# Four of an expert's twelve weight chunks kept in a second place, loaded one expert ahead and moved by VectorE

## The chip, the cores and the metric

The kernel runs on one core of a Trainium2 chip. The metric is the device time of one execution in microseconds (us). The core has five engines with their own instruction streams: TensorE (PE; its weight loads are listed as PEld), VectorE (DVE), ScalarE (ACT), GpSimd (POOL) and SyncE (SP). They run side by side and meet at semaphores. Transfers are carried by 16 DMA engines; SP, ACT and POOL issue them.

## The reference

A transformer block with a mixture of experts, followed by a second block with two kinds of attention, on 512 tokens of width 1024, all in float32. Only the mixture of experts matters here:

```python
logits = (xt @ p['w_router'] + p['b_router']).astype(F32)   # 512 tokens, 32 experts
top_val, top_idx = lax.top_k(logits, TOP_K)                 # TOP_K = 4
gates = jax.nn.softmax(top_val, axis=-1)
...
def expert_block(args):
    e, x_b = args
    gu = x_b @ w_gu[e] + b_gu[e]                            # 1024 x 2048
    gate = jnp.minimum(gu[..., ::2], SWIGLU_LIMIT)
    up = jnp.clip(gu[..., 1::2], -SWIGLU_LIMIT, SWIGLU_LIMIT)
    return ((up + 1.0) * (gate * jax.nn.sigmoid(SWIGLU_ALPHA * gate))) @ w_dn[e] + b_dn[e]
```

Each token goes through four of the 32 experts, and the four results are summed with the gates as weights.

## The kernel before

**Blocks.** The kernel works on blocks of 64 token slots (`SLOTS`), each of one expert. An expert with more than 64 tokens has two or more blocks, one behind the other. The routing stage (`route_stage`, a chain of small VectorE operations) counts the tokens of each expert, orders the experts so that large and small ones alternate as evenly as they can, and writes a table: the expert of block v. For these inputs there are 47 blocks, and the numbers of blocks of the experts in their order are 1, 2, 1, 1, 2, 1, 2, 1, 1, 2, 1, 1, 2, 1, 2, 1, 1, 2, 1, 1, 4, 1, 2, 1, 1, 2, 1, 1, 3, 1, 2, 1: twelve experts with more than one block, twenty with one. (Blocks are counted from 1 in this document.)

**Weights.** An expert's weights are 12 MB, twelve chunks of 1 MB: 0 to 7 for gate and up (0 to 3 for half 0 of the columns, 4 to 7 for half 1), 8 to 11 for down. SBUF has room for one expert, one place for each chunk (`expert_w`). There is one semaphore `chunk{i}_arrived` for each chunk.

**The loop** (`experts`, stage `moe`). Each engine has a loop over the blocks, and `takes(engine, signal, n)` waits for a signal and takes it away again.

- SP (L1320 to 1327): for chunks 0 to 11, in this order, it waits until TensorE has used the chunk in this block, and then issues the load of the same chunk of the next block's expert. Where the next block has the same expert, the load is skipped and only its signal is given:

```python
for i in range(CHUNKS):
    takes(sp, s["last_used"] if i == CHUNKS - 1 else s["used"])
    sp.dma_start(w[:, i], weights.source[after, i], cond=(after != here)).then_inc(arrived[i], 16)
```

- TensorE (L1342 to 1393): gate and up, half 0 and half 1, chunk by chunk, each behind its `arrived` (L1353); the turn of the activation of half 0 (L1365) and of the next block's tokens (L1274); the down product of half 0 with chunks 8 and 9 (L1379); the turn of half 1 and its down product with chunks 10 and 11. The turns use the gated activation that VectorE makes.
- VectorE (L1433 to 1445): it spreads the bias with a shuffle (L1435), and for each half adds it to the product (L1439), clips, and multiplies gate and up with ScalarE's sigmoid into `act_sb` (L1445).
- ScalarE: the sigmoid (L1400), which loads its table in the first half; copies of the turned activation (L1404); the modulation of the next block's tokens (L1280); the copy of the down result `yb` (L1421) and its store; the load of the next bias.
- GpSimd: the gather of the next block's tokens (L1335).

The first expert's chunks are called for in the stage `ffn` (`load_first`), before the routing.

Of the kernel before, what the change touches and what calls it, by code (L numbers as in the profile page):

```python
# [15 lines left out]
F32 = mybir.dt.float32  # L16
# [6 lines left out]
P = 128  # L23
# [145 lines left out]
class LateModulation:  # L169
# [5 lines left out]
    def __init__(self, nc, held, ones):  # L175
        self.nc, self.ones = nc, ones
        self.cond = held.enter_context(nc.sbuf_tensor("late_cond_cols", [P, LATE, KD], F32))
        self.columns = held.enter_context(nc.sbuf_tensor("late_columns", [P, LATE * 4], F32))
# [454 lines left out]
def ffn_block(nc, d, g, ring, x, row_cols, ones):  # L633

    tiles = [x[:, m] for m in range(NT_X)]
    with ExitStack() as ffn:
        def sb(name, shape, dtype=F32):
            return ffn.enter_context(nc.sbuf_tensor(name, shape, dtype))

        gain, shift = sb("ffn_gain", [P, KD]), sb("ffn_shift", [P, KD])  # L640
        weight, slot_of = sb("weight_of", [P, NT_X, TOP_K]), sb("slot_of", [P, NT_X, TOP_K], U32)
        of_expert = sb("of_expert", [P, NT_X, N_EXP])
        token_of = sb("token_of", [P, LISTED], U32)
        table, n_blocks = sb("table", [1, P], I32), sb("n_blocks", [1, 1], I32)
        rows = nc.dram_tensor("normed_rows", (SEQ, D), F32).ap()
        y = sb("ffn_y", [P, NT_X, D])
        moving = ffn.enter_context(ExitStack())
        weights = ExpertWeights(nc, d, moving)
        routing = ffn.enter_context(ExitStack())
        hT = routing.enter_context(nc.sbuf_tensor("ffn_hT", [P, KD, SEQ], F32))  # L650
# [11 lines left out]
        norm_turn_stage(nc, "ffn", tiles, None, [y[:, m] for m in range(NT_X)], hT,  # L662
                        lambda m, k: (gain[:, k:k + 1], shift[:, k:k + 1]), g.eps_col[:, 0:1], g.ident[:, :],
                        early=weights.load_first)
        route_stage(nc, tables, g, hT, ones, y, rows, weight, slot_of, of_expert, token_of, table, n_blocks)
        routing.close()
        slot_rows = experts(nc, d, g, weights, rows, gain, shift, token_of, table, n_blocks)
        moving.close()
        combine(nc, d, g, slot_rows, weight, slot_of, of_expert, y)
        row = sb("ffn_row", [P, D])  # L670
        rows_stage(nc, g, "ffn_rows", [row_cols[:, 1]], [row[:, :]], ones)
        add_normed_stage(nc, g, "post_ffn", [y[:, m] for m in range(NT_X)], tiles, row[:, :],
                         early=lambda sp: ring.call_first(sp, second_weights(d)))

# [306 lines left out]
CHUNKS = 12  # L981
LIMIT, ALPHA = 7.0, 1.702
# [22 lines left out]
def route_stage(nc, tables, g, hT, ones, xn, rows, weight, slot_of, of_expert, token_of, table, n_blocks):  # L1005
# [6 lines left out]
    with ExitStack() as held:  # L1012
        def sb(name, shape, dtype=F32):
            return held.enter_context(nc.sbuf_tensor(name, shape, dtype))
# [27 lines left out]
        experti = sb("router_experti", [P, 1], I32)  # L1042
        ps = held.enter_context(nc.psum_tensor("router_ps", [P, NT_X, 512], F32))
        ps_r = held.enter_context(nc.psum_tensor("router_rank", [P, 1, 512], F32))
        with stage(nc, "route", "by_expert", "by_expert_kept", "logits", "negtop", "weight", "chosen", "rank", "chain", "expert",
                   "table", "slots", "hot", "listed", "rows", "at", "top", clear=(tables.loaded,)) as (s, block):
            @block.sync
            def _(sp):
                sp.wait_ge(s["expert"], 2)
                sp.dma_start(table[0:1, :], experti[:, 0:1]).then_inc(s["table"], 16)  # L1050
                sp.wait_ge(s["table"], 16)
# [43 lines left out]
            def _(dve):  # L1095
# [62 lines left out]
                step(nc.vector.tensor_scalar(many[:, 2:3], many[:, 2:3], -1.0, part[:, 0:1], ALU.add, ALU.min))  # L1158
# [5 lines left out]
                nc.vector.tensor_copy(experti[:, :], expert[:, 0:1]).then_inc(s["expert"], 1)  # L1164
# [65 lines left out]

def experts(nc, d, g, weights, rows, gain, shift, token_of, table, n_blocks):
# [9 lines left out]
    with ExitStack() as held:  # L1241
# [22 lines left out]
        carried = [stored, bias_here, gu_read, xg_free, xgT_made]  # L1264
# [20 lines left out]

        with stage(nc, "moe_start", "tokens", "xg_turned", "set", "rows_set", pool_dma=(gathered,)) as (s, block):
            @block.vector
            def _(dve):
                nc.vector.tensor_copy(tokens[:, :], token_of[:, 0:1]).then_inc(s["tokens"], 1)
                nc.vector.memset(yb[:, 0:1], 0.0).then_inc(gu_read, 2)  # L1290
                nc.vector.memset(yb[:, 1:2], 0.0).then_inc(stored, 32)
                nc.vector.memset(b_rows[:, :], 0.0).then_inc(s["rows_set"], 1)
# [21 lines left out]
        with stage(nc, "moe", "used", "last_used", "gu_made", "bias_free", "ga", "sig", "acted", "turned", "actT",  # L1314
                   "dn_made", "yb_made", "xg_here", "xg_turned", "copied", "step", pool_dma=(gathered,)) as (s, block):

            def takes(engine, signal, n=1):
                engine.wait_ge(signal, n).then_inc(signal, -n)  # L1318

            @block.sync  # L1320
            def _(sp):
                with sp.Fori(0, turns) as v:
                    here = sp.value_load(table[0:1, bass.ds(v, 1)], min_val=0, max_val=N_EXP - 1)
                    after = sp.value_load(table[0:1, bass.ds(v + 1, 1)], min_val=0, max_val=N_EXP - 1)
# [19 lines left out]
            def _(pe):  # L1344
# [26 lines left out]
                def down(half):  # L1371
                    takes(pe, s["actT"])
                    for q in range(2):
                        i = 8 + 2 * half + q
                        takes(pe, arrived[i], 16)
# [7 lines left out]
                        last.then_inc(s["used"] if i < CHUNKS - 1 else s["dn_made"], 1)  # L1383
# [13 lines left out]
            def _(act):  # L1397
# [9 lines left out]
                with act.Fori(0, turns) as v:  # L1407
                    here = act.value_load(table[0:1, bass.ds(v, 1)], min_val=0, max_val=N_EXP - 1)
                    after = act.value_load(table[0:1, bass.ds(v + 1, 1)], min_val=0, max_val=N_EXP - 1)
# [9 lines left out]
                    nc.scalar.sem_inc(s["last_used"], 1)  # L1419
# [8 lines left out]
            def _(dve):  # L1428
# [4 lines left out]
                with dve.Fori(0, turns):  # L1433
# [1473 lines left out]
def build_program(nc, d, out):  # L2907
    with ExitStack() as whole:
# [48 lines left out]
        ring = WeightRing(nc, "b2_w", whole)  # L2957
        ffn_block(nc, d, g, ring, x, row_cols, ones[:, :])
# [163 lines left out]
```

## Time and profile before

| | |
|---|---|
| runs | 3132.25 us median of 3 (3132.21 to 3143.58) |
| the profiled execution's own time | 3136.93 us |
| its span in the trace | 3135.1 us |
| granted TensorE clock, mean over the span | 0.912 |
| TensorE matmuls busy | 2613.1 us (83%) |
| VectorE busy | 1013.8 us (32%) |
| expert loop, from its first matmul to the last read of the down result | 1286.8 to 2436.2 us |
| bytes moved by DMA over the whole span | 553.36 MB |

The span runs from the first to the last instruction of one profiled execution. Busy shares are means over stages with different limits, so what matters for a change in the expert loop is read from the loop's own rows. In the rows further down, a timeline row gives the start, the length, the engine, the line and the operation; "x64" is the number of instructions merged, and the brackets tell how long the engine had been idle before and what ended that.

### The profile page before, as it was taken

What the parts mean: (1) busy time and instruction counts of PE and PEld (TensorE: products, weight loads), DVE (VectorE), ACT (ScalarE), POOL (GpSimd) and SP (SyncE); (2) the same over time, 40 slices, a digit from 0 to 9 for tenths busy, and PEclk for the clock granted to TensorE, in tenths of its full rate; (3) what the DMA queues carried; (4) which work ended last, traced back from release to release, by engine and by line L of the source; (5) the groups of instructions that cost most, each with busy time, mean ns of one, the idle gap of its engine ahead of it and who ended that gap; (6) DMA issues with size and microseconds to landing.
All of it is one profiled execution on the core that took longest, in us unless ns stands there. A gap on an engine that the chain in (4) does not pass through costs nothing. (4 is left out here: it accounts for less than half of the span.)

```text
span 3135.1 us, 51899 instructions
## 1 busy us (share of the span) xinstructions
PE 2613.1 (83%) x19294; PEld 1299.5 (41%) x19294; DVE 1013.8 (32%) x2284; ACT 764.4 (24%) x1726; POOL 346.5 (11%) x331
## 2 busy tenths in 40 slices
PE   6788686856789994699988989998999399679998
PEld 1446464645464442333333333333333154355444
DVE  1263636363155424322222222222222502443012
ACT  2133333343060002122222222222222201355000
POOL 0021212130060000000000000000000201244000
PEclk9888798977889997799999999999999599887999
DMA  5100000000307414499999999399968421001112
GB/s 203 57 26 23 6 23 6 23 2 3 108 28 281 147 67 183 184 390 387 387 391 390 387 395 422 150 384 411 402 269 360 148 90 64 19 2 55 54 56 79
DMA packets 114086, 553.36 MB, mean 177 GB/s; under 512 B 12912, under 2 KB 16496, under 8 KB 62352
## 3 DMA queue, kind: packets, MB, share of 16 engines
q1 hardware_dynamic: 97184, 510.27, 40.4%
q10 hardware_dynamic: 10608, 19.91, 1.9%
q0 software_dynamic: 6144, 20.98, 1.8%
q8 instruction: 119, 1.95, 0.3%
q14 instruction: 31, 0.25, 0.0%
HBM read 736.18 MB, written 16.52 MB: 240 GB/s over the span
## 5 line engine op out<-in xcount | busy, mean ns | idle before, releaser
L1353 PE MATMUL moe_gu_ps<-expert_w,xgT 128*64 128x512 f32 x3008 | 667.9, 595 | 39.3 <-PEq L1318 39.2
L1353 PEld LDWEIGHTS moe_gu_ps<-expert_w,xgT 128*64 128x64 f32 x3008 | 252.8, 137 | 445.5 <-issue 445.5
L1379 PE MATMUL moe_down_ps<-expert_w,actT 128*64 128x512 f32 x1504 | 344.6, 597 | 54.8 <-PEq L1318 54.8
L1439 DVE TENSOR_TENSOR biased<-moe_gu_ps,b_gu 128x512 f32<-128x512 f32 x94 | 65.0, 692 | 615.7 <-DVEq L1318 615.7
L1379 PEld LDWEIGHTS moe_down_ps<-expert_w,actT 128*64 128x64 f32 x1504 | 116.7, 136 | 222.2 <-issue 222.2
L1400 ACT ACT_TABLE_LOAD x47 | 60.3, 1283 | 383.0 <-ACTq L1318 383.0
L1868 PE MATMUL ahead_ps<-hT,x 128*128 128x256 f32 (+1 forms) x288 | 128.1, 542 | 5.8 <-PEq L57 5.8
L1280 ACT ACTIVATE xgT<-moe_xg_ps,ffn_shift,ffn_gain 128x64 f32<-128x64 f32 x384 | 119.2, 424 | 41.0 <-PE moe_xg_ps L1274 41.0
L1404 ACT COPY actT<-moe_act_ps 128x256 f32<-128x256 f32 x94 | 35.0, 373 | 375.9 <-ACTq L1318 375.9
L1333 POOL COPY tokens<-token_of 128x1 uint32 x47 | 8.6, 183 | 1040.7 <-POOLq L1318 1040.7
L386 PE MATMUL b2p_ps<-b_w,b_hT 128*128 128x512 f32 (+1 forms) x320 | 119.4, 535 | 1.9 <-PEq L57 1.9
L386 PE MATMUL gates_ps<-mix_w,hT 128*128 128x512 f32 x256 | 112.6, 596 | 0.7 <-PEq L57 0.7
L386 PE MATMUL b2g_ps<-b_w,b_hT 128*128 128x512 f32 x256 | 110.1, 592 | 0.7 <-PEq L57 0.7
L386 PEld LDWEIGHTS b2p_ps<-b_w,b_hT 128*128 128x128 f32 x320 | 57.8, 190 | 63.4 <-issue 63.4
L386 PEld LDWEIGHTS b2g_ps<-b_w,b_hT 128*128 128x128 f32 x256 | 48.6, 190 | 61.6 <-issue 61.6
L522 POOL TENSOR_SCALAR window_prob<-window_prob,window_col 128x512 f32<-128x512 f32 (+1 forms) x32 | 54.8, 1726 | 168.4 <-DVE window_col L507 168.4
L386 PEld LDWEIGHTS gates_ps<-mix_w,hT 128*128 128x128 f32 x256 | 47.8, 190 | 56.8 <-issue 56.8
L386 PE MATMUL proj_ps<-mix_w,hT 128*128 128x256 f32 (+1 forms) x160 | 51.5, 486 | 21.1 <-DMA mix_w<-in_w_in_tok 21.1
L2188 POOL TENSOR_TENSOR aoff<-gb,solve_masks 128x512 f32<-128x512 f32 x45 | 57.2, 1287 | 93.0 <-PE solve_ps L2013 53.3
L1705 POOL TENSOR_TENSOR f_k<-f_k 128x768 f32<-128x768 f32 x8 | 17.0, 2148 | 444.7 <-ACT f_k L1741 444.7
L214 DVE SCALAR_TENSOR_TENSOR late_sums<-late_w,late_cond_cols,late_sums 128x512 f32<-128x512 f32 x84 | 63.1, 751 | 2.6
L1435 DVE STREAM_SHUFFLE b_gu<-b_rows 128x1024 f32<-128x1024 f32 x47 | 62.2, 1322 | 0.4
(690 smaller groups left out, 3721.6 us busy)
## 6 DMA issues: line engine op xcount, KB each, us to landing
expert_w<-in_w_experts SPq DMA_DIRECT2D x576, 1024.0 KB
late_w<-in_w_late SPq DMA_DIRECT2D x12, 2048.0 KB, 8.4
b_w<-in_w_in SPq DMA_DIRECT2D x10, 2048.0 KB, 7.6
ada_w<-in_w_ada SPq DMA_DIRECT2D x6, 2048.0 KB, 12.4
slot_rows<-yb ACTq DMA_DIRECT2D x94, 128.0 KB, 6.2
mix_w<-in_w_in_tok SPq DMA_DIRECT2D x5, 2048.0 KB, 9.9
x<-in_w_rkv SPq DMA_DIRECT2D x5, 1536.0 KB, 7.6
mix_w<-in_w_out SPq DMA_DIRECT2D x2, 2048.0 KB, 7.7
```

The source lines that it names most:

```text
L214: nc.vector.scalar_tensor_tensor(out, w, c, out, ALU.mult, ALU.add).then_inc(s["late_sum"], 1)
L386: last = nc.tensor.matmul(ps[:, t % 4, 0:chunk["width"]], chunk["lhs"][m](k), ring.slot(c)[:, k, 0:chunk["width"]], start=start, stop=stop)
L522: nc.gpsimd.tensor_scalar(prob[:, p % 3, j, 0:wide(p)], prob[:, p % 3, j, 0:wide(p)], c(p, INV, j), None, ALU.mult).then_inc(s["shared"], 1)
L1280: last = nc.scalar.activation(xgT[:, k, :], ps_xg[:, k % 4, at:at + SLOTS], ACT.Identity, scale=gain[:, k:k + 1], bias=shift[:, k:k + 1])
L1353: last = nc.tensor.matmul(ps_gu[SLOTS * j:SLOTS * j + SLOTS, half, :], xgT[:, k, :], w[:, i, at:at + 512], start=(k == 0), stop=(k == KD - 1),
L1379: last = nc.tensor.matmul(ps_dn[SLOTS * j:SLOTS * j + SLOTS, :], actT[:, half, q, SLOTS * a:SLOTS * a + SLOTS], w[:, i, at:at + 512], star ...
L1400: nc.scalar.activation(sg[:, :], ga[:, :], ACT.Sigmoid, scale=ALPHA).then_inc(s["sig"], 1)
L1404: nc.scalar.copy(actT[:, half, :, :], ps_act[:, half, 0:256].rearrange("p (q t) -> p q t", q=2)) \
L1435: step(nc.vector.stream_shuffle(b_gu[:, :, :].rearrange("p h n -> p (h n)"), b_rows[:, :], [0] * 32))
L1439: step(nc.vector.tensor_tensor(biased[:, :], ps_gu[:, half, :], b_gu[:, half, :], ALU.add))
L1868: last = self.nc.tensor.matmul(self.ps[:, group % 2, 0:n], self.w[:, k, i * P:(i + 1) * P], self.hT[:, k, lo:lo + n], start=(k == 0), stop ...
L2188: nc.gpsimd.tensor_tensor(flat(m.aoff[:, l % 2]), m.gb[:, :, :, 0, :].rearrange("p a q t -> p (a q) t"), eight(masks[:, 2 + l, :]), ALU.mu ...
```

## The change

Four places are added to `expert_w`: 12 to 15. Gate and up chunks keep their places 0 to 7. A down chunk now is loaded into place 12 to 15 (`STAGED` = 4), and VectorE copies it, 128 x 2048 elements for each chunk, into place 8 to 11 at the beginning of a block, once the block before has finished its down product (`down_free`). TensorE's down product waits for `chunk_moved` in place of `arrived`. In a block that isn't the first of its expert the copy goes from the second place onto itself.

SP now issues in the order 0, 1, down 0, 2, 3, down 1, 4, 5, down 2, 6, 7, down 3. The eight others are called for in the last block of an expert, as before. The four down chunks of the next expert are called for in the *first* block of an expert, each when VectorE has moved the one in its place (`stage_free`). In an expert with only one block both happen in that block. On VectorE the four waits and copies stand ahead of the shuffle of the bias. The routing stage writes two more rows of the table, for which it has ten more small operations: the expert whose down chunks are to be called for in block v, and the place that the copies of block v go to (8 or 12).

To make room, the ring of the second block's weights and `ffn_y` are allocated only after the experts, the normed tokens get a tensor of their own (`ffn_xn`), and `of_expert` shares room with an earlier table.

```diff
+STAGED = 4
+KEPT = CHUNKS - STAGED
...
             def _(sp):
                 sp.wait_ge(s["expert"], 2)
-                sp.dma_start(table[0:1, :], experti[:, 0:1]).then_inc(s["table"], 16)
-                sp.wait_ge(s["table"], 16)
+                for j in range(3):
+                    sp.dma_start(table[0:1, j, :], experti[:, j:j + 1]).then_inc(s["table"], 16)
+                sp.wait_ge(s["table"], 48)
...
-                step(nc.vector.tensor_scalar(many[:, 2:3], many[:, 2:3], -1.0, part[:, 0:1], ALU.add, ALU.min))
+                last_block = many[:, 3:4]
+                step(nc.vector.tensor_scalar(last_block, many[:, 2:3], -1.0, None, ALU.add))
+                step(nc.vector.tensor_scalar(many[:, 2:3], last_block, part[:, 0:1], None, ALU.min))
...
-                nc.vector.tensor_copy(experti[:, :], expert[:, 0:1]).then_inc(s["expert"], 1)
+
+                step(nc.vector.scalar_tensor_tensor(tmp[:, :], starts[:, :], part[:, 0:1], ends[:, :], ALU.is_equal, ALU.mult))
+                step(nc.vector.tensor_reduce(many[:, 0:1], tmp[:, :], AX.X, ALU.max))
+                step(nc.vector.tensor_scalar(many[:, 1:2], many[:, 0:1], 0.5, -float(STAGED), ALU.is_gt, ALU.mult))
+                step(nc.vector.tensor_scalar(expert[:, 2:3], many[:, 1:2], float(CHUNKS), None, ALU.add))
+                step(nc.vector.tensor_tensor(many[:, 0:1], many[:, 0:1], part[:, 0:1], ALU.max))
+                step(nc.vector.tensor_scalar(many[:, 0:1], many[:, 0:1], last_block, None, ALU.min))
+                step(nc.vector.scalar_tensor_tensor(tmp[:, :], starts[:, :], many[:, 0:1], iota[:, 0:N_EXP],
+                                                    ALU.is_le, ALU.mult))
+                step(nc.vector.scalar_tensor_tensor(tmp[:, :], ends[:, :], many[:, 0:1], tmp[:, :], ALU.is_gt, ALU.mult))
+                step(nc.vector.tensor_reduce(expert[:, 1:2], tmp[:, :], AX.X, ALU.add))
+                nc.vector.tensor_copy(experti[:, :], expert[:, 0:3]).then_inc(s["expert"], 1)
...
-        self.w = held.enter_context(nc.sbuf_tensor("expert_w", [P, CHUNKS, 2 * D], F32))
+        self.w = held.enter_context(nc.sbuf_tensor("expert_w", [P, CHUNKS + STAGED, 2 * D], F32))
...
         for i in range(CHUNKS):
-            sp.dma_start(self.w[:, i], self.source[0, i]).then_inc(self.arrived[i], 16)
+            place = i if i < KEPT else STAGED + i
+            sp.dma_start(self.w[:, place], self.source[0, i]).then_inc(self.arrived[i], 16)
...
-                    for i in range(CHUNKS):
-                        takes(sp, s["last_used"] if i == CHUNKS - 1 else s["used"])
-                        sp.dma_start(w[:, i], weights.source[after, i], cond=(after != here)).then_inc(arrived[i], 16)
...
+                    following = sp.value_load(table[0:1, 1, bass.ds(v, 1)], min_val=0, max_val=N_EXP - 1)
+                    for i in range(STAGED):
+                        for q in (2 * i, 2 * i + 1):
+                            takes(sp, s["used"])
+                            sp.dma_start(w[:, q], weights.source[after, q], cond=(after != here)).then_inc(arrived[q], 16)
+                        takes(sp, stage_free)
+                        sp.dma_start(w[:, CHUNKS + i], weights.source[following, KEPT + i],
+                                     cond=(following != here)).then_inc(arrived[KEPT + i], 16)
...
-                        takes(pe, arrived[i], 16)
+                        takes(pe, moved)
...
                     takes(act, s["dn_made"])
-                    nc.scalar.sem_inc(s["last_used"], 1)
+                    nc.scalar.sem_inc(down_free, 1)
...
-                with dve.Fori(0, turns):
+                with dve.Fori(0, turns) as v:
+                    to = dve.value_load(table[0:1, 2, bass.ds(v, 1)], min_val=KEPT, max_val=CHUNKS)
+                    takes(dve, down_free)
+                    for i in range(STAGED):
+                        takes(dve, arrived[KEPT + i], 16)
+                        step(nc.vector.tensor_copy(w[:, bass.ds(to + i, 1), :], w[:, CHUNKS + i:CHUNKS + i + 1, :]))
+                        nc.vector.sem_inc(moved, 1)
+                        nc.vector.sem_inc(stage_free, 1)
                     takes(dve, bias_here, 32)
```

## Rows read from the trace of the kernel before

**Rows 1.** The page: TensorE's busy tenths and the DMA engines' in 40 slices.
```profile
PE   6788686856789994699988989998999399679998
...
DMA  5100000000307414499999999399968421001112
```

**Rows 2.** Windows, one per block: length, busy us by engine, clock, DMA share, GB/s.
```profile
1336.20:1359.60 23.40, 22.24 (x108) 8.92 (x106) 5.39 (x12) 5.85 (x15) 1.16 (x2) 1.00 0.91 365
...
1406.30:1436.70 30.40, 24.27 (x108) 8.00 (x108) 5.41 (x12) 5.88 (x15) 1.16 (x2) 1.00 0.92 381
...
1947.80:1977.80 30.00, 23.95 (x108) 7.85 (x106) 5.45 (x12) 5.83 (x14) 1.16 (x2) 1.00 0.92 385
...
2165.00:2195.50 30.50, 24.38 (x107) 8.07 (x109) 5.40 (x12) 5.82 (x14) 1.16 (x2) 1.00 0.93 387
```

**Rows 3.** Timeline of TensorE, blocks 4 and 6.
```profile
1359.08 13.93 PE L1353 MATMUL moe_gu_ps<-expert_w,xgT 128*64 128x512 f32 x64
...
1408.98 1.94 PE L1353 MATMUL moe_gu_ps<-expert_w,xgT 128*64 128x512 f32 x8 [0.88 <-PEq L1318]
...
1417.29 1.94 PE L1353 MATMUL moe_gu_ps<-expert_w,xgT 128*64 128x512 f32 x8 [0.38 <-PEq L1318]
...
1424.66 1.94 PE L1353 MATMUL moe_gu_ps<-expert_w,xgT 128*64 128x512 f32 x8 [0.56 <-PEq L1318]
1426.53 0.44 PE L1365 MATMUL moe_act_ps<-ident,act_sb 128*128 128x128 f32 x2
```

**Rows 4.** Windows: blocks 3 to 6 together; one microsecond (its last two: DMA, GB/s).
```profile
1338.00:1433.00 95.00, 85.25 (x394) 32.24 (x391) 21.66 (x48) 21.02 (x50) 3.60 (x7) 1.00 1.00 417
...
1350.00:1351.00 1.00, 1.00 1.09 459
```

**Rows 5.** Timeline of all engines in block 21.
```profile
1800.43 13.93 PE L1353 MATMUL moe_gu_ps<-expert_w,xgT 128*64 128x512 f32 x64
...
1800.92 0.59 ACT L1421 COPY yb<-moe_down_ps 128x512 f32<-128x512 f32 x1 [1.86 <-ACTq L1318]
...
1807.64 0.69 DVE L1439 TENSOR_TENSOR biased<-moe_gu_ps,b_gu 128x512 f32<-128x512 f32 x1 [7.18 <-DVEq L1318]
...
1808.58 0.29 DVE L1441 TENSOR_SCALAR ga<-biased 128x256 f32<-128x256 f32 x1 [0.24 <-DVEq L1318]
...
1810.85 0.43 DVE L1445 TENSOR_TENSOR act_sb<-up,sg 128x256 f32<-128x256 f32 x1 [1.20 <-DVEq L1318]
...
1814.29 0.44 PE L1365 MATMUL moe_act_ps<-ident,act_sb 128*128 128x128 f32 x2
```

**Rows 6.** Groups of VectorE's instructions by line and shape.
```profile
L1435 DVE STREAM_SHUFFLE b_gu<-b_rows 128x1024 f32<-128x1024 f32 x47 | 62.2, 1322 | 0.4
...
L2141 DVE COPY added<-solve_ps 128x512 f32<-128x512 f32 x9 | 6.2, 692 | 16.4 <-PE solve_ps L2013 16.2
...
L211 DVE TENSOR_SCALAR late_sums<-late_w,late_cond_cols 128x512 f32<-128x512 f32 x12 | 5.8, 480 | 1.7 <-DMA late_w<-in_w_late 1.6
...
L281 DVE TENSOR_SCALAR pre_xn<-pre_x,pre_stat 128x1024 f32<-128x1024 f32 x4 | 3.0, 754 | 0.1
```

**Rows 7.** Windows of 1 us on TensorE: length, busy us, clock, DMA, GB/s.
```profile
169.00:170.00 1.00, 0.80 (x2) 1.00 0.00 0
...
174.00:175.00 1.00, 0.00 (x0) 0.99 0.00 0
...
181.00:182.00 1.00, 1.00 (x3) 0.60 0.00 0
...
1192.00:1193.00 1.00, 0.37 (x1) 1.00 0.00 0
...
1195.00:1196.00 1.00, 0.00 (x0) 0.78 0.00 0
...
1291.00:1292.00 1.00, 1.00 (x7) 0.93 0.49 57
```

**Rows 8.** Timeline of VectorE in the routing stage.
```profile
1256.74 0.19 DVE L1160 TENSOR_TENSOR router_tmp<-router_tmp,router_iota 128x32 f32<-128x32 f32 x1
```

More of the change, by code:

```diff
@@ L630, in _, with ffn_block @@
             nc.vector.tensor_copy(row_cols[:, 2, :], g.ada2[:, 16:24, 0]).then_inc(s["done"], 1)
-def ffn_block(nc, d, g, ring, x, row_cols, ones):
+def ffn_block(nc, d, g, whole, room, x, row_cols, ones):
     tiles = [x[:, m] for m in range(NT_X)]
@@ L661, in _ @@
                 nc.vector.tensor_copy(shift[:, :], g.ada[:, 24:32, 0]).then_inc(s["done"], 1)
-        norm_turn_stage(nc, "ffn", tiles, None, [y[:, m] for m in range(NT_X)], hT,
+        norm_turn_stage(nc, "ffn", tiles, None, [xn[:, m] for m in range(NT_X)], hT,
                         lambda m, k: (gain[:, k:k + 1], shift[:, k:k + 1]), g.eps_col[:, 0:1], g.ident[:, :],
                         early=weights.load_first)
-        route_stage(nc, tables, g, hT, ones, y, rows, weight, slot_of, of_expert, token_of, table, n_blocks)
+        route_stage(nc, tables, g, hT, ones, xn, rows, weight, slot_of, of_expert, token_of, table, n_blocks)
         routing.close()
@@ L668, in ffn_block @@
         moving.close()
+        ring = WeightRing(nc, "b2_w", whole)
+        y = ffn.enter_context(nc.sbuf_tensor("ffn_y", [P, NT_X, D], F32))
         combine(nc, d, g, slot_rows, weight, slot_of, of_expert, y)
-        row = sb("ffn_row", [P, D])
+        row = ffn.enter_context(nc.sbuf_tensor("ffn_row", [P, D], F32))
         rows_stage(nc, g, "ffn_rows", [row_cols[:, 1]], [row[:, :]], ones)
@@ L673, in ffn_block @@
                          early=lambda sp: ring.call_first(sp, second_weights(d)))
+    return ring
 def mix_inputs(nc, d, g, hT):
@@ L1284, in modulate, with takes @@
             last.then_inc(xgT_made, 1)
+        def takes(engine, signal, n=1):
+            engine.wait_ge(signal, n).then_inc(signal, -n)
         with stage(nc, "moe_start", "tokens", "xg_turned", "set", "rows_set", pool_dma=(gathered,)) as (s, block):
@@ L1313, in experts @@
         turns = nc.values_load(n_blocks[0:1, 0:1], min_val=N_EXP, max_val=MAX_BLOCKS)
-        with stage(nc, "moe", "used", "last_used", "gu_made", "bias_free", "ga", "sig", "acted", "turned", "actT",
+        with stage(nc, "moe", "used", "gu_made", "bias_free", "ga", "sig", "acted", "turned", "actT",
                    "dn_made", "yb_made", "xg_here", "xg_turned", "copied", "step", pool_dma=(gathered,)) as (s, block):
-            def takes(engine, signal, n=1):
-                engine.wait_ge(signal, n).then_inc(signal, -n)
             @block.sync
@@ L1407, in _ @@
                 with act.Fori(0, turns) as v:
-                    here = act.value_load(table[0:1, bass.ds(v, 1)], min_val=0, max_val=N_EXP - 1)
-                    after = act.value_load(table[0:1, bass.ds(v + 1, 1)], min_val=0, max_val=N_EXP - 1)
+                    here = act.value_load(table[0:1, 0, bass.ds(v, 1)], min_val=0, max_val=N_EXP - 1)
+                    after = act.value_load(table[0:1, 0, bass.ds(v + 1, 1)], min_val=0, max_val=N_EXP - 1)
                     sigmoid()
@@ L2956, in build_program @@
         mixing_block(nc, d, g, late, x, row_cols, ones[:, :])
-        ring = WeightRing(nc, "b2_w", whole)
-        ffn_block(nc, d, g, ring, x, row_cols, ones[:, :])
+        ring = ffn_block(nc, d, g, whole, late.room, x, row_cols, ones[:, :])
         second_block(nc, d, g, ring, x, row_cols, ones[:, :], out)
```

32 lines of the change are left out of this document (19 added, 13 removed).

## The prediction, made before the changed kernel was run

> **What bounds the kernel now.** I read the page first: TensorE is busy 83% of the span, and the slices show a stretch in which the DMA engines also stand at nine tenths or more [rows 1]. That stretch is the expert loop. I cut it at the block ends (one window per block, 47 of them). A block takes 23.4 us, and seven take 30.4, 30.3, 30.0, 30.0, 30.0, 30.5 and 30.2 us (three of the seven stand in [rows 2]): 211.4 less 7 x 23.4 is 47.6 us. By the order of the experts' blocks (the kernel before), these are blocks 6, 13, 17, 24, 28, 37 and 41: each is the first block after two one-block experts in a row. The timeline of TensorE shows what a long block is: the matmuls of each 1 MB chunk start a little late, one chunk after the other, about 2.46 us apart at the end where they need 1.74 [rows 3]. So they wait for weights.
>
> How fast weights come: between 1338 and 1433 us the DMA engines are busy all the time [rows 4]. Its 95 us at 417 GB/s are 39.6 MB: the 36 chunks of three experts (37.7 MB) and the gathers and stores of the blocks. That is 2.64 us a chunk and 31.7 us an expert. A block after which the expert changes lasts 23.4 us, so each one-block expert makes the loads 8.3 us later; a second block of the same expert calls for nothing and lets them catch up. Before, one such lag is hidden in full, since chunk 11 is needed only 20 us into its block; two in a row are not.
>
> **What the change does to the loads.** The bytes are the same. In the first block of a two-block expert the four down chunks of the next expert are loaded, which was idle DMA time; its last block then calls for eight chunks (21 us, under the 23.4). But in the only block of a one-block expert all twelve are still called for, in the order 0, 1, down 0, 2, 3, down 1, 4, 5, down 2, 6, 7, down 3. So the last to land is a down chunk, and VectorE now waits for it at the *head* of the next block, before it spreads the bias, adds it and makes the activation. What was needed last is now asked for first, and everything of VectorE's block is queued behind it.
>
> **When it lands.** Chunk 7 of block 6 lets its matmuls go at 1424.66 [rows 3]; chunk 11 is four later, 4 x 2.46, so 1434.5. Two experts earlier (24 x 2.64 = 63.4) gives 1371.1 for the twelfth chunk of the expert of block 4, whose matmuls began at 1359.08 [rows 3]: 12.0 us into the block. It was the same number of bytes from the same starting point (a block that follows a two-block expert), so this is the arrival of the last down chunk after the change as well.
>
> **What follows on VectorE.** Offsets are from the first gate-up matmuls of a block (1800.43) [rows 5]. The bias add starts at +7.2, the activation of half 0 is done at +10.85 (3.64 us after the add starts), TensorE turns it at +13.86: 3.0 us in hand. The down result is read at +0.5, so about there the moves may begin.
>
> The trace has no VectorE copy of 128x2048 from SBUF to SBUF. Lower bound: the one-source operation on 128x1024 takes 754 ns and on 128x512 480 ns [rows 6]; continued by the same slope, 2048 takes 1.30 us. Upper bound: a copy out of PSUM takes 692 ns for 512 and the shuffle 1322 for 1024 [rows 6]; at that rate 2048 takes 2.4 us. I take 1.30, since this copy has source and result where the 754 ns row has them. With the gap that a waited step leaves (1808.33 to 1808.58, 0.25) a move is 1.55. The Trainium skill, "VectorE: DVE Perf Modes", section "The perf-mode tier table", gives an fp32 tensor_copy of 2048 within SBUF the doubled rate, 1227 ns, and only any PSUM operand or a shuffle the single one; by it the last move ends 0.07 us earlier, and the sum changes by under 1 us. By a single-rate copy the sum would be the rival below.
>
> *Blocks where the chunks have landed* (28 of 47): moves +0.5 to +6.7, shuffle with its gap 1.6 to +8.3, activation done at +11.95, still 1.9 before TensorE asks. Cost nothing, hidden by the gate-up matmuls; if a move with its gap took over 2.0 us this cover would be gone. This holds for the repeat blocks too, where the copy goes onto itself.
>
> *First block after a one-block expert that followed a longer one*: last chunk at +12.0, move 1.55, shuffle 1.6, chain 3.64, signal 0.1: +18.9 instead of +13.86, a stall of 5.0 us in one piece. Half 1's activation follows in 2.7 us, while TensorE does the first down half, so it adds nothing.
>
> *The clock.* Waits before were a few tenths to 1.2 us and the granted clock stayed at 1.00 in every block [rows 2]. A lump is another thing: TensorE stopped at 1192.4 and the clock fell from 1.00 to 0.50 (2.4 to 1.2 GHz) within 1195 to 1196 [rows 7]; after the stop at 169.8 it held until 175 [rows 7], the longest of eight such pauses. When the loop began at 1286.8 at half clock, the full one came back at 1291.1, after 4.3 us of work; after the work that began at 175.6 it was 181.4, 5.8 us [rows 7]. Work at half clock loses half its time: 2.2 us is my value for a stall, bounds 0 and 2.9. The Trainium skill, "TensorE: Matmul & The Clock Gate", section "HAM oscillation — how this bites in real kernels", has a kernel that pays this anew at each wait for weights; the trace agrees that a pause brings it, and by a clock that holds the sum is the first rival.
>
> *After two one-block experts in a row* the second first-block gets its chunk at 12.0 + 31.7 - (23.4 + 5.0 + 2.2) = +13.1: stall 6.1, clock 2.2, together 8.3. The pair costs 7.2 + 8.3 = 15.5.
>
> **The sum.** Seven pairs and five single places (blocks 2, 9, 20, 33, 45; the expert of block 1 also has one block, and its loads begin at 1290.9, so 31.7 + 1.6 later is again about +12): 7 x 15.5 + 5 x 7.2 = 144.5 us. Removed: 47.6. The routing stage gets ten more small VectorE operations of 0.19 and a gap of 0.04 each [rows 8], in a chain that ends in the gather TensorE waits for: + 2.3. The two more table DMAs lie beside 18 us of that chain: 0. Moving the ring, x and y within SBUF adds no work: 0. Net +99.2. The profiled execution took 3136.93 (span 3135.1), so 3236.1; the median of the runs is 4.7 below it: **3231 us**.
>
> **Rivals.** *The clock holds, or comes back at once*: for it, the fall once took 5.2 us (169.8 to 175) and the stall is 5.0; against it, the clock was down at the end of each of the eight pauses. Single 5.0, pair 13.3: 118.1, net +72.8, 3205 us. *The copy runs at the single rate* (2.65 a move): 28 covered blocks stall 2.6 each, singles cost 5.7, pairs 14.0, since the longer block before gives the loads time: 199.3, net +154, 3286 us. For it only that no such copy is in the trace. *The other side, faster*: 31 experts' loads are 31 x 31.7 = 983 us, less than the loop's 47 x 23.4 + 47.6 = 1147, so on average they fit, and half the one-block experts gain idle time ahead of them. If the last down chunk landed by +6.9 (6.9 + 1.55 + 1.6 + 3.64 = 13.7), no block would wait: -47.6 + 2.3, 3087 us. That is the point from which it decides; it would need the twelve chunks in 26.6 us for 31.7, which is 417 x 31.7 / 26.6 = 497 GB/s, where the fastest single microsecond of that stretch had 459 [rows 4]. *No change*: first-block lag hidden by something I overlooked and pairs costing their 8.3: 7 x 8.3 = 58.1, net +13, 3145 us.
>
> **How the numbers follow.** My forecast 0.70 (its own range, c from 1.5 to 2.9 and the arrival 1 us either way at 12 places: 3212 to 3250), clock holds 0.12, single-rate copy 0.05, faster 0.05, about the same 0.04 (some of it under, some over the bound), other slower mixtures 0.04. Range 3200 to 3255. What a measurement of this kernel can tell from no change is about 0.5%, 16 us. Faster 0.05, same 0.04, slower 0.91.
>
> **What would show it.** TensorE's turn of the activation (L1365 before the change) idles 5 to 6 us in 19 blocks, always in first blocks after one-block experts, never in gate-up, with the granted clock under 1.00 in those blocks; VectorE's move of the last down chunk starts there about 12 us into the block; moves take 1.2 to 1.3 us; blocks that follow a two-block expert stay at 23.4; the routing is 2 to 3 us longer. I am wrong if those turns do not wait, if moves take over 2 us, or if the last down chunk lands before +7.

## The result, and the profile after

| | before | after |
|---|---|---|
| runs, median (lowest to highest) | 3133.96 us (3132.21 to 3143.58), 4 runs | 3245.31 us (3238.30 to 3261.60), 4 runs |
| ratio, 95% interval | | 1.0356 (1.0331 to 1.0381) |
| the profiled execution's span | 3135.1 us | 3236.2 us |
| loop, first matmul to last read of the down result | 1149.3 us | 1257.0 us |
| blocks over 23.6 us (the first, 26.0 and 26.2 us, left out) | 7, excess over 23.4 together 47.6 us | 19, excess 155.1 us |

The change makes the kernel 3.6% slower; 3231 us was forecast. A block's length is counted from one read of the down result to the next. The windows of blocks 4 to 7 answer to [rows 2] (length, busy us of TensorE, its weight loads, VectorE, ScalarE and GpSimd, clock, DMA share, GB/s):

```profile
1359.10:1382.50 23.40, 22.24 (x108) 8.88 (x106) 10.30 (x16) 5.82 (x15) 1.16 (x2) 1.00 0.97 387
1382.50:1414.00 31.50, 23.94 (x108) 9.49 (x106) 10.19 (x16) 5.78 (x14) 1.16 (x2) 0.89 1.01 421
1414.00:1444.90 30.90, 23.70 (x107) 9.42 (x105) 10.19 (x16) 5.78 (x14) 1.16 (x2) 0.89 0.74 300
1444.90:1468.30 23.40, 22.24 (x108) 8.94 (x106) 10.30 (x16) 5.82 (x14) 1.16 (x2) 1.00 0.90 352
```

Block 5 is the first block after a one-block expert, block 6 the first after two. Both are long now, and their clock is under 1.00. The two others show that four more copies on VectorE (10.3 us busy for 5.4) can cost a block nothing. What happens in block 5 is in its timeline (start, length, engine, line, operation):

```profile
1382.00 13.93 PE L1383 MATMUL moe_gu_ps<-expert_w,xgT 128*64 128x512 f32 x64
1382.49 0.58 ACT L1452 COPY yb<-moe_down_ps 128x512 f32<-128x512 f32 x1 [1.88 <-ACTq L1311]
1382.68 1.23 DVE L1469 COPY expert_w<-expert_w 128x2048 f32 x1 [7.29 <-DVEq L1311]
...
1384.45 1.23 DVE L1469 COPY expert_w<-expert_w 128x2048 f32 x1 [0.55 <-DVEq L1311]
1387.51 1.23 DVE L1469 COPY expert_w<-expert_w 128x2048 f32 x1 [1.82 <-DVEq L1311]
1395.58 1.23 DVE L1469 COPY expert_w<-expert_w 128x2048 f32 x1 [6.84 <-DVEq L1311]
...
1397.28 1.29 DVE L1473 STREAM_SHUFFLE b_gu<-b_rows 128x1024 f32<-128x1024 f32 x1
1398.91 0.69 DVE L1477 TENSOR_TENSOR biased<-moe_gu_ps,b_gu 128x512 f32<-128x512 f32 x1 [0.35 <-DVEq L1311]
...
1402.12 0.42 DVE L1483 TENSOR_TENSOR act_sb<-up,sg 128x256 f32<-128x256 f32 x1 [1.20 <-DVEq L1311]
...
1402.69 0.66 PE L1395 MATMUL moe_act_ps<-ident,act_sb 128*128 128x128 f32 x2 [6.76 <-PEq L1311]
1403.15 1.06 PE L1298 MATMUL moe_xg_ps<-ident,xg 128*128 128x128 f32 x4
...
1404.15 4.74 PE L1409 MATMUL moe_down_ps<-expert_w,actT 128*64 128x512 f32 x16
```

The gate-up matmuls run through in 13.93 us, with all their weights there. VectorE stands 6.84 us before its fourth copy, which starts 13.58 us into the block; only then come the shuffle, the bias add (13.58 + 3.33) and the activation. TensorE idles 6.76 us before it can turn it. The bracket names only VectorE's own queue. That the wait is for the fourth chunk follows from the code, where nothing else can hold that copy up, and is tested below. All of TensorE's waits of this kind are one row of the list of waits (engine, line, waited for: us, times, longest):

```profile
PE moe_act_ps L1395 <- PEq L1311: 127.7, 19, 7.2
```

Nineteen times, 6.7 us each (6.0 to 7.2). No gate-up matmul of these 19 blocks waits. And the pause costs a second time (windows of 1 us of block 5: length, TensorE's busy us, clock, DMA share, GB/s):

```profile
1395.00:1396.00 1.00, 0.93 (x6) 1.00 0.98 410
...
1399.00:1400.00 1.00, 0.00 (x0) 0.77 0.99 410
...
1405.00:1406.00 1.00, 1.00 (x6) 0.50 1.02 426
1406.00:1407.00 1.00, 1.00 (x7) 0.81 1.03 426
```

TensorE stops at 1395.9, the granted clock falls from 1.00 to 0.50 (from 2.4 to 1.2 GHz) within 1399 to 1400, and is back within 1406 to 1407, after the work that began at 1402.7. In between the two turns take 0.66 us for 0.44, the tokens' 1.06 for 0.60, and the first down half 4.74 for 3.65.

The copies are one group of the page:

```profile
L1469 DVE COPY expert_w<-expert_w 128x2048 f32 x188 | 230.7, 1227 | 600.3 <-DVEq L1311 600.3
```

### The profile page after: what moved, and what is told of

The parts are those of the page before. It is cut to its first block and busy times, and to the rows that moved or that the text cites. A ratio compares the mean times of both kernels' runs of the same rounds, so it can differ in the third digit from the quotient of the medians.

```text
span 3236.2 us, 53553 instructions
## 1 busy us (share of the span) xinstructions
PE 2630.5 (81%) x19294; PEld 1316.7 (41%) x19294; DVE 1243.6 (38%) x2484; ACT 763.1 (24%) x1726; POOL 346.5 (11%) x331
## 5 line engine op out<-in xcount | busy, mean ns | idle before, releaser
L1383 PE MATMUL moe_gu_ps<-expert_w,xgT 128*64 128x512 f32 x3008 | 657.2, 594 | 4.4 <-PEq L1311 4.4
L1469 DVE COPY expert_w<-expert_w 128x2048 f32 x188 | 230.7, 1227 | 600.3 <-DVEq L1311 600.3
L1409 PE MATMUL moe_down_ps<-expert_w,actT 128*64 128x512 f32 x1504 | 365.9, 629 | 47.6 <-PEq L1311 47.6
L1395 PE MATMUL moe_act_ps<-ident,act_sb 128*128 128x128 f32 x188 | 45.4, 327 | 127.7 <-PEq L1311 127.7
L1395 PEld LDWEIGHTS moe_act_ps<-ident,act_sb 128*128 128x128 f32 x188 | 20.5, 153 | 204.7 <-issue 204.7
```

What stands on the lines that cost most here:

```text
L1383: last = nc.tensor.matmul(ps_gu[SLOTS * j:SLOTS * j + SLOTS, half, :], xgT[:, k, :], w[:, i, at:at + 512], start=(k == 0), stop=(k == KD - 1),
L1395: last = nc.tensor.transpose(ps_act[:, half, j * P:(j + 1) * P], act_sb[:, half, j * P:(j + 1) * P], ident)
L1409: last = nc.tensor.matmul(ps_dn[SLOTS * j:SLOTS * j + SLOTS, :], actT[:, half, q, SLOTS * a:SLOTS * a + SLOTS], w[:, i, at:at + 512], star ...
L1469: step(nc.vector.tensor_copy(w[:, bass.ds(to + i, 1), :], w[:, CHUNKS + i:CHUNKS + i + 1, :]))
```

## The experiments

Eight kernels ran, one of them twice. Each is compared with its own runs of the kernel before on the same chip. The lengths below are from their traces: the mean over the five single places (blocks 2, 9, 20, 33, 45), the seven firsts of a pair (5, 12, 16, 23, 27, 36, 40) and the seven seconds (6, 13, 17, 24, 28, 37, 41). Offsets count from the block's first gate-up matmul. "Last copy" is its start, so an upper bound for the landing of its chunk, and "turn" is TensorE's first turn of the activation, at +13.86 where nothing waits.

```
                 single / first / second, us   last copy, first   turn, first   loop, us
before            23.4    23.4    30.2          none               13.86        1149.3
after             31.8    31.7    31.3          13.67              20.78        1257.0
order_only        32.5    32.3    31.5          14.09              21.21        1266.8
small_copies      31.2    31.6    31.0          13.84              19.90        1251.9
one_late          23.4    23.4    31.0          16.68              13.86        1154.8
downs_first       27.6    28.2    31.5           5.99              18.68        1213.6
late_moves        23.4    23.4    27.1          18.56              13.86        1127.7
copies_only       23.9    24.7    30.9          none needed        14.25        1166.7
copies_no_read    23.5    23.8    31.0          none needed        13.90        1158.5
turn_between      32.3    32.0    31.8          13.20              20.41        1277.7
```

**order_only: the order of SP alone.**

```diff
-                    for i in range(STAGED):
-                        for q in (2 * i, 2 * i + 1):
-                            takes(sp, s["used"])
-                            sp.dma_start(w[:, q], ...)
-                        takes(sp, stage_free)
-                        sp.dma_start(w[:, CHUNKS + i], ...)
+                    for q in range(KEPT):
+                        takes(sp, s["used"])
+                        sp.dma_start(w[:, q], ...)
+                    for i in range(STAGED):
+                        takes(sp, stage_free)
+                        sp.dma_start(w[:, CHUNKS + i], ...)
```

> The changed kernel with one edit: SP asks for chunks 0 to 7 first and for the four down chunks behind them, no longer in between. VectorE's waits and copies stay at the head of the block. Theory (VectorE waits at the head for the chunk that lands last): the last of twelve is a down chunk in either order, so the last copy still starts about 13.7 us into the block and the stalls at the turn of the activation stay at 6.5 to 7 us in the same 19 blocks: 3235 to 3255 us. Rival (the interleaved order delays the gate and up chunks, and that is the loss): chunk 7 now lands four chunks earlier and the loss shrinks by a third or more, 3205 us or less.

Measured: 3247.08 us (3243.72 to 3260.60), ratio to before 1.0375 (1.0343 to 1.0407). The last copy starts at +14.1, the turn at +21.2. That is 116.0 us above its own before, where the changed kernel was 111.4 above: interleaving isn't the loss. A down chunk is last in either order.

**late_moves: VectorE's waits and copies behind its activations.** Besides the edit of order_only:

```diff
-                    for i in range(STAGED):
-                        takes(dve, arrived[KEPT + i], 16)
-                        step(nc.vector.tensor_copy(w[:, bass.ds(to + i, 1), :], w[:, CHUNKS + i:CHUNKS + i + 1, :]))
-                        ...
                     for half in range(2):
                         ...
                         nc.vector.tensor_tensor(act_sb[:, half, :], up[:, :], sg[:, :], ALU.mult).then_inc(s["acted"], 1)
+                        for i in (2 * half, 2 * half + 1):
+                            takes(dve, arrived[KEPT + i], 16)
+                            step(nc.vector.tensor_copy(w[:, bass.ds(to + i, 1), :], w[:, CHUNKS + i:CHUNKS + i + 1, :]))
+                            ...
```

> As order_only, and in addition the waits and copies of the down chunks no longer stand at VectorE's head: those of chunks 8 and 9 stand behind the activation of half 0, those of 10 and 11 behind that of half 1. Theory: the twelve single and first places lose their whole stall (the last chunk, there at +13.7, is needed at about +18), and the seven second places keep 2 to 4 us each, because the last chunk lands there at 13.7 + 31.5 - 23.4 = +21.8 and is to be copied by +21.7: loop excess 14 to 28 us where before had 47.6, so 3105 to 3125 us, faster than before. Rival (the copies themselves, or the double traffic in SBUF, cost the time): as slow as the changed kernel, over 3200 us. Rival (loads simply don't fit, whoever waits): 7 x 8.3 = 58 us of excess, 3145 us.

Measured: 3113.90 us (3109.45 to 3115.05) beside 3131.06, ratio 0.9938 (0.9921 to 0.9956): faster than the kernel before. The same bytes are loaded and copied. All twelve single and first places are back at 23.4 us. The seven seconds keep 2.7 to 4.9 us: four of them 2.7 to 3.2, and three (blocks 13, 17 and 37) 4.6 to 4.9, the three in which the granted clock fell to 0.50 for 3.4 us. Block 6, VectorE and TensorE:

```profile
1410.89 0.43 DVE L1478 TENSOR_TENSOR act_sb<-up,sg 128x256 f32<-128x256 f32 x1 [1.20 <-DVEq L1311]
1414.33 0.44 PE L1395 MATMUL moe_act_ps<-ident,act_sb 128*128 128x128 f32 x2
1414.89 1.23 DVE L1481 COPY expert_w<-expert_w 128x2048 f32 x1 [3.58 <-DVEq L1311]
...
1417.37 1.23 DVE L1481 COPY expert_w<-expert_w 128x2048 f32 x1 [1.26 <-DVEq L1311]
...
1421.30 0.43 DVE L1478 TENSOR_TENSOR act_sb<-up,sg 128x256 f32<-128x256 f32 x1 [0.26 <-DVEq L1311]
...
1421.88 0.41 PE L1395 MATMUL moe_act_ps<-ident,act_sb 128*128 128x128 f32 x2 [1.04 <-PEq L1311]
```

The activation of half 0 is ready at 1411.3, 3.0 us before TensorE turns it. The copies wait for their chunks (3.58 and 1.26 us), and the activation of half 1 is now queued behind them: the same mistake in small, which costs 1.0 us at the second turn besides the later chunks.

**small_copies: the waits without the work.** `tensor_copy(w[:, bass.ds(to + i, 1), 0:2], w[:, CHUNKS + i:CHUNKS + i + 1, 0:2])`

> The changed kernel with copies of 2 columns in place of 2048; all waits, signals and loads stay. It leaves out the moving of the down weights: the down product runs with a constant 0.01 in places 8 to 11, set once ahead of the loop (4 to 9 us). Theory (the wait is the loss, the copy only adds its own length behind it): the covered blocks stay at 23.4; the stalls of the twelve singles and firsts shrink by the 1.2 us of the one copy behind the last landing, those of the seven seconds hardly, being set by the loads: loop 12 to 20 us shorter than in the changed kernel, 3230 to 3240 us in all. Rival (230 us of copies on VectorE are the loss): the 19 long blocks come down to 25 us or less and the time to 3160 us or less.

Measured: 3247.24 us (3243.80 to 3250.44), ratio 1.0369 (1.0350 to 1.0388). That is 7 us above the theory's range, which counted the fill (it took 6.9 us), and 87 us above the rival's. The loop is 5.1 us shorter, where 12 to 20 were expected: a miss in size. The wait in first places shrank by 0.9 us (turn at +19.90 for +20.78), but what comes behind it grew from 1.4 to 2.1 us, and the last chunk wasn't earlier. The clock fits the growth: it came back 4.3 to 5.7 us after work resumed in 18 of the 19 places, and in the changed kernel after 3.1 to 4.3 us in 16 of them. The verdict between the two stands: with the 231 us of copies nearly gone, the 19 blocks are still 30 to 32 us long.

**copies_only: the work without the waits.** Loads, places and waits of the kernel before, four copies at VectorE's head:

```diff
+                    for i in range(0, STAGED):
+                        step(nc.vector.tensor_copy(w[:, CHUNKS + (i + 2) % 4:CHUNKS + (i + 2) % 4 + 1, :], w[:, CHUNKS + i:CHUNKS + i + 1, :]))
```

> The kernel before in its loads, places and waits, with the four copies of 128x2048 put at the head of each block on VectorE, between the four spare places, which nothing else reads; the routing's ten operations and the two table transfers stay too, and a fill of the spare places adds 4 to 9 us once ahead of the loop. Theory (the copies are covered): every block that took 23.4 us takes 23.4, the seven long ones 30 to 31, total 3134 + 4 to 9 = 3136 to 3145 us. Rival (the copies slow TensorE's operands or the transfers): blocks over 23.6 us, or a transfer rate under 417 GB/s in the stretch of three one-block loads, 3160 us or more.

Measured: 3165.68 us (3162.41 to 3168.06), ratio 1.0110 (1.0093 to 1.0127). A miss: 20 us above the upper end of the theory and inside the rival's range, so this run by itself did not clear the copies. Blocks that wait for nothing did keep 23.4 us, but the first places came out at 24.7 and the seconds at 30.9. SP's issues showed a difference that I had left in by mistake: the read of the table's second row at the head of its loop. Outside the second places, the first load of a block went out +3.82 to +4.03 us after the first gate-up matmul, in the kernel before +2.83 to +3.19 (the next expectation counts 0.08 us less for this run).

**copies_no_read: the same without that read.**

> As copies_only, without the one table read that had stayed at the head of SP's loop (the third, which only the changed kernel needs). In copies_only SP issued the first load of a block at +3.75 to +3.94, in the kernel before at +2.83 to +3.12. Theory (that read delays the first load by 0.9 us, the copies delay nothing): first loads go back to +2.8 to +3.1, the loop is within 3 us of the 1149.3 us of the kernel before (copies_only: 1166.7), and the total, with the fill of the spare places ahead of the loop, falls by 14 to 18 us to 3147 to 3152 us. Rival (VectorE's copies slow SP's issue or the transfers): first loads stay at +3.7 or the loop over 1160 us.

Measured: 3153.70 us (3148.83 to 3165.11), ratio 1.0053 (1.0032 to 1.0073). First loads are at +2.91 to +3.27, so the read was their delay but for 0.08 us. Two of the seven first places are back at 23.4 us; the others take 23.8 to 24.1. The loop is 1158.5 us, 9.2 above before and outside both ranges, and the median is 1.7 us above the theory's: the firsts add 2.9 us, the seconds 5.5 (31.0 for 30.2 us each). Counted from the first load of seven runs of loads, the bytes moved in 33 us lie within 0.17 MB of the kernel before's, some above and some below; after 65 us this one is 59 to 225 KB behind in six, up to 0.5 us of transfer, and 14 KB ahead in one. So the copies take little from the transfers, and why the loop is 9 us longer stays open; it is a twelfth of the loss in question. The 17.7 us by which the median is above before's are about the fill's 6.9, the routing's 2.3 and these 9.2.

**one_late: one wait of the four.** In the changed kernel, only the wait and copy of the last down chunk go behind half 1's activation; SP's order isn't touched.

```diff
-                    for i in range(STAGED):
+                    for i in range(STAGED - 1):
                         takes(dve, arrived[KEPT + i], 16)
                         ...
                     for half in range(2):
                         ...
+                    i = STAGED - 1
+                    takes(dve, arrived[KEPT + i], 16)
+                    step(nc.vector.tensor_copy(...))
```

> The changed kernel with one of VectorE's four waits and copies moved: that of the last down chunk stands behind the activation of half 1; the other three stay at the head, and SP's order stays as it is. Theory (the wait for the chunk that lands last, put ahead of the block's activations, is the loss): the other three have landed by +5.5 in the twelve single and first places, so these go back to 23.4 us; the seven second places stay long by 7 to 8.3 us, since chunk 7 lands there at about +18.9 and is needed at +12.2, and the third down chunk lands at +13.6: excess 49 to 58 us, 3130 to 3150 us. Rival (the sum of waits, copies and staging costs, not one wait): at most a quarter of the loss goes, 3210 us or more.

Measured: 3139.65 us (3137.31 to 3153.80, 10 runs) beside 3136.05, ratio 1.0023 (1.0008 to 1.0037). Moving this one wait leaves 3.6 us of the 111.4. All twelve single and first places are at 23.4 us; the excess of the seconds is 53.3 us. In block 6 the wait has gone to gate-up, as worked out:

```profile
1424.29 1.94 PE L1383 MATMUL moe_gu_ps<-expert_w,xgT 128*64 128x512 f32 x8 [0.36 <-PEq L1311]
1429.26 1.94 PE L1383 MATMUL moe_gu_ps<-expert_w,xgT 128*64 128x512 f32 x8 [3.03 <-PEq L1311]
1431.75 1.94 PE L1383 MATMUL moe_gu_ps<-expert_w,xgT 128*64 128x512 f32 x8 [0.55 <-PEq L1311]
1434.03 0.41 PE L1395 MATMUL moe_act_ps<-ident,act_sb 128*128 128x128 f32 x2 [0.34 <-PEq L1311]
```

**downs_first: the order turned round.** SP calls for the four down chunks ahead of chunks 0 to 7; VectorE as in the changed kernel.

> The changed kernel with SP asking for the four down chunks first and for chunks 0 to 7 behind them; VectorE is untouched. Theory (what counts is when the last chunk lands against when it is needed): the last to land is now chunk 7, needed at +12.2 by TensorE and not at the head by VectorE, so nothing waits at the head. In single and first places chunk 7 lands 1 to 2.5 us late, in the second places 7.5 to 8 us late, in small waits without the fall of the clock: excess 65 to 90 us where the changed kernel has 155, 3150 to 3180 us. Rival (any staging behind VectorE costs this much, in whatever order): 3235 us or more.

Measured: 3198.34 us (3196.26 to 3211.68), ratio 1.0198 (1.0178 to 1.0218). The direction is the theory's: all four copies start by +6.0 in every block, nothing waits at VectorE's head, and TensorE waits in gate-up (3.5 to 3.7 us in eleven of the twelve single and first places, 6.4 in the seconds). The granted clock doesn't fall anywhere in the loop. But it is 18 us above the range. First and single places are 4.8 and 4.2 us late where I had 1 to 2.5: SP's loads of chunks 0 to 7 now queue behind its waits for VectorE's copies, even in blocks where it needs none of them. In the last block of an expert with several, chunk 0 is called for at +8.29, where the changed kernel had +2.35.

**turn_between: does a little work keep the clock?** TensorE turns the next block's tokens in the middle of its pause, released by VectorE after the shuffle.

> The changed kernel with the turn of the next block's tokens moved ahead of the turn of half 0's activation on TensorE, and behind a signal that VectorE gives when it has spread the bias. In the 19 long blocks that is about 3 us into TensorE's pause and 4 us before its end, 0.6 us of work; everything else waits as before. Theory (of the 8.3 us of a long block 6.9 are the wait and 1.4 the half clock behind it): if the work in between keeps the clock up, long blocks get 0.8 to 1.4 us shorter and TensorE's two turns take 0.44 again; the wait itself stays at 6.5 to 7.5 us. In covered blocks the turn of the activation goes 0.3 to 0.6 us later, 28 times: in sum within 20 us of the changed kernel's 3245. Rival (the clock falls anyway): long blocks stay at 31 to 32 us with a granted clock of 0.5 at the resumption, total 3245 to 3265 us.

Measured: 3271.94 us (3265.00 to 3277.73), ratio 1.0430 (1.0392 to 1.0469): a little above the rival's range. Block 5 has the first pause cut in two (2.43 and 3.21 us), and the clock falls anyway, 1 us after the work in between:

```profile
1408.33 0.63 PE L1298 MATMUL moe_xg_ps<-ident,xg 128*128 128x128 f32 x4 [2.43 <-PEq L1311]
1412.17 0.66 PE L1395 MATMUL moe_act_ps<-ident,act_sb 128*128 128x128 f32 x2 [3.21 <-PEq L1311]
1413.63 5.17 PE L1409 MATMUL moe_down_ps<-expert_w,actT 128*64 128x512 f32 x16 [0.79 <-PEq L1311]
```
```profile
1409.00:1410.00 1.00, 0.00 (x0) 0.94 0.98 410
1410.00:1411.00 1.00, 0.00 (x0) 0.50 1.00 418
```

The clock fell in all 19 places. It also came back later, 4.1 to 9.6 us after the activation's turn began: what is lost behind the wait is 2.1 to 2.5 us here, for 1.4 in the changed kernel, and the covered blocks are 0.4 us longer.

**late_moves_again.**

> The same kernel as late_moves, on another chip beside its own runs of the kernel before, to narrow the interval of the ratio: 0.992 to 0.996 expected. If the gain were chance of that chip or that day, the ratio would be within 0.3% of 1.

Measured: 3111.71 us (3103.89 to 3118.65, 6 runs) beside 3134.75, ratio 0.9920 (0.9891 to 0.9948). The gain holds on a second chip. That this kernel has the change's other parts too (the new places, the routing, the later ring) and is faster than before rules them out as the loss.

## Why the prediction was right, step by step

| term | forecast | trace |
|---|---|---|
| long blocks, and which | 19 | the same 19 |
| a move | 1.30 + 0.25 gap | 1.23 + 0.55 gap |
| covered blocks | +0 | +0 in 27 of 28; the first block of all 26.2 for 26.0 |
| last down chunk in single and first places | +12.0 | +13.67 |
| from there to the turn | 6.9 | 7.1 |
| wait of TensorE there | 5.0 | 6.9 |
| clock behind it | 2.2 | 1.4 |
| single or first place together | 7.2 | 8.4 |
| second place together | 8.3 | 7.9 |
| all stalls | 144.5 | 155.1 |
| stalls of before that go | 47.6 | 47.6 |
| routing | +2.3 | +2.30 |
| sum | +99.2 | +109.8; medians +111.4 |

**The mechanism** is shown. The head-of-block wait is on the path (timeline, list of waits), and it carries nearly all of the loss: order_only leaves it and the time stays, small_copies takes the copies and the time stays, one_late moves a single wait and 108 of 111 us go. The seconds were long before the change (30.2 us, now 31.3), so 100 us of the loss are in the twelve single and first places. TensorE waits longer than the prediction's own sign said (6.0 to 7.2 us, not 5 to 6), in the places and at the turn that it named.

**Part of the closeness is luck.** The prediction bounded its two main terms, the landing by 1 us either way of +12.0 and the clock's price by 1.5 to 2.9 us. Both came out beyond these bounds, the one late and the other cheap, and in opposite directions. With the landing as measured and 2.2 us for the clock, its own sum gives 165.0 us of stalls and 3252 us, just inside the range.

**Routing.** From the first count matmul to the one that follows VectorE's chain: 1243.38 to 1268.41 before, 1232.98 to 1260.31 after, 25.03 and 27.33 us.

```profile
1232.98 0.80 PE L1074 MATMUL router_rank<-router_chosen,router_before 128*128 128x128 f32 x2 [4.32 <-DVE router_chosen L1128]
...
1260.31 1.97 PE L1087 MATMUL router_ps<-router_of_block,router_in_block 128*128 128x65 f32 x8 [23.71 <-DVE slot_of L1231]
```

**The mis-sized term is the landing of the last chunk**, +12.0 for +13.67. I had gone back from the end of a run of 36 chunks with its *mean* of 2.64 us. But the run starts slowly. Windows of the kernel before, and of the changed one:

```profile
1338.00:1341.00 3.00, 3.00 (x18) 1.00 0.76 202
1341.00:1344.00 3.00, 3.00 (x18) 1.00 1.02 423
...
1338.00:1371.00 33.00, 31.84 (x152) 1.00 0.99 402
```
```profile
1361.00:1364.00 3.00, 3.00 (x16) 1.00 0.81 209
1364.00:1367.00 3.00, 3.00 (x16) 1.00 1.00 410
```

The first 3 us bring half of what the later ones do. That slow start belongs to the first twelve chunks alone, so their last one lands later than the mean says, and the two next experts' sooner. By bytes: 33 us at 402 GB/s are 13.3 MB up to 1371, the 12.6 MB of twelve chunks and their share of gather and store. From a chunk's last bytes to its matmuls some 1.8 us pass: the transfers are over by 1432.7, so chunk 7's bytes were there four chunks of 2.46 us earlier, at 1422.9, and its matmuls began at 1424.66 [rows 3]. By this estimate the twelfth chunk is there at 1372.8, +13.7. That it is the places coming free one by one which slows the start (the second load goes out 1.2 us after the first in the kernel before, 1.7 in the changed one) fits, but no run tests it. Twelve places at 1.7 us are 20 us, and the chain behind the landing adds 0.2 us to each; the cheaper clock took back 10 us there, and the second places came out 3 us below.

**The clock** cost 1.4 us a stall, not 2.2. It fell in every one of the 19 pauses, 2.6 to 4.9 us after TensorE stopped. It came back 3.1 to 5.9 us after work resumed, 3.9 in the mean, where the forecast went by 4.3 and 5.8; the trace of the kernel before also has a return after 2.8 us (the pause that ends at 76.6) and one after 3.1 (at 69.5). Part of that time were gaps in which TensorE had no work to lose. The Trainium skill, "TensorE: Matmul & The Clock Gate", section "HAM oscillation — how this bites in real kernels", tells of a matmul kernel that waits for its next slice of data again and again and starts at the lower clock after each wait; here the trace agrees in all 19 places. In the loop of the kernel before, whose waits are 0.4 to 1.2 us each, the clock never fell. The rival "the clock holds" fell.

**The other rivals.** The single-rate copy: 1227 ns was measured, as the Trainium skill, "VectorE: DVE Perf Modes", section "The perf-mode tier table", has it. The slack of the covered blocks was thinner than I said, 0.9 us for 1.9, because each move leaves a gap of 0.55 and not 0.25. The wait for a DMA's signal and two more signals stand in it; in copies_no_read, without them, the gap is 0.15. The upper bound was also misworked: continued from the rows it used (692 ns for 512, 1322 for 1024), 2048 takes 2.6 us and not 2.4. The faster case failed at the point named: the chunk lands at +13.7, it needed +6.9. Its reasoning (on average the loads fit) was true, and late_moves is what it looks like once the wait is where the data is needed.

**Between the profiles.** The spans differ by 101.1 us and not 110, since the changed kernel's profiled execution was the quickest of its four and had come to the routing 10.4 us sooner (first router matmul at 1220.54 for 1230.94). That is scatter between executions: the six other traces with the same kernel up to there come to it between 1222.3 and 1235.2.

## What to carry to other kernels

A wait stands ahead of everything behind it in that engine's order. Before putting one at the head of an iteration, ask when its data lands *in the worst iteration*, and what is queued behind it that doesn't need that data. Here chunks used late in a block, the last of them 20 us into it, were awaited at its beginning. That turned a prefetch that gains 0.6 to 0.8% into a loss of 3.6%, and with the last chunk's wait alone moved away, 0.2% of it were left.

When transfers and compute are nearly as long, go through the real order of the work and not the average: the loads take 983 us in a loop of 1149, and yet two one-block experts in a row make every following chunk late. A lag worked back from the end of a burst needs the slow start of the burst taken out first.

To tell a wait from its work, take each alone: the tiny copy said in one run that the copies weren't the loss. The copy without a wait needed a second, because the first had a stray read in it and landed in the rival's range.

## What the runs showed of the hardware that I had not expected

- The clock fell in a pause that was cut by 0.63 us of TensorE's work: 2.43 us idle, the work, and the clock at 0.50 some 1 us later, still at 0.50 when work resumed 3.2 us after it.
- Short pauses can bring it down too. In late_moves blocks 13, 17 and 37 had a pause of 1.4 us and one of 1.0 us some 5.5 us apart, the clock fell to 0.50 for 3.4 us, and they were 28.0 to 28.3 us long. Blocks 24 and 28, with nearly the same two pauses (1.3 to 1.4 and 1.0), kept the clock and took 26.3 to 26.6.
- One more register read of a table in SBUF at the head of SP's loop sent a block's first load out 0.9 us later (+3.83 for +2.91), and put 8 us on the loop (1166.7 for 1158.5). In the changed kernel, which has the same read but whose SP is done with the block before in time, the first load goes out at +2.35.
- A copy of 128x2 elements within SBUF took 0.17 us and its step another 0.55 us of gap: four of them are nearly 3 us, without any data to speak of.
